# A feed-forward stage's second product: its first three row units taken one after another instead of together

## What is computed

```
def macaron_half_ffn(x, pre_g, post_g, w_gate, w_up, w_down):
    h = rmsnorm(x, pre_g)
    h = (jax.nn.silu(h @ w_gate) * (h @ w_up)) @ w_down
    return x + 0.5 * rmsnorm(h, post_g)

def swiglu_ffn(x, w_in, w_out):
    gate, up = jnp.split(x @ w_in, 2, axis=-1)
    return (jax.nn.silu(gate) * up) @ w_out
```

## Time and profile before

| what | value |
|---|---|
| time, median of 3 runs | 3608.6 us (3608.32 to 3608.63) |
| time of the profiled execution | 3610.27 us |
| its span, first to last instruction | 3608.5 us |
| PE busy with matmuls | 3288.3 us (91%) |
| DVE, ACT, POOL busy | 52%, 42%, 25% |
| mean granted TensorE clock | 0.927 of full speed |
| bytes read from HBM | 479.27 MB, 133 GB/s over the span |

### The profile page before, as it was taken

The page is one execution under the profiler, slowest core; times in us unless marked ns, Lnnn a source line. Parts: engine busy times, 40 slices in busy tenths (PEclk is TensorE's granted clock), DMA queues, the critical chain, the costliest instruction groups (busy, mean ns, idle before and its releaser), DMA issues.

```text
span 3608.5 us, 63629 instructions
## 1 busy us (share of the span) xinstructions
PE 3288.3 (91%) x27126; PEld 3135.9 (87%) x27126; DVE 1860.2 (52%) x3109; ACT 1514.5 (42%) x2540; POOL 915.4 (25%) x522
## 2 busy tenths in 40 slices
PE   7998999998798999979978999999899979987998
PEld 7997899996687999978858899899789979975898
DVE  4546455547664554365565344454435545454453
ACT  4444444444223444446454444443334443433342
POOL 2221223232342232312212222223122222220222
PEclk9998999998898999989979999999899989986899
DMA  5542354554102545533413345354224534520353
GB/s 204 175 162 80 119 185 150 185 167 148 60 3 94 181 158 187 181 127 112 138 68 129 129 152 187 133 174 152 88 82 147 175 106 153 175 86 20 107 175 117
DMA packets 133242, 484.44 MB, mean 134 GB/s; under 512 B 14815, under 2 KB 17007, under 8 KB 132255
## 3 DMA queue, kind: packets, MB, share of 16 engines
q1 hardware_dynamic: 130976, 470.25, 38.9%
q0 software_dynamic: 1984, 10.12, 0.8%
HBM read 479.27 MB, written 1.05 MB: 133 GB/s over the span
## 4 chain that ended last, share of the span: by engine, by line
PE 66%; DVE 13%; ACT 11%; issue 9%; POOL 1%; DMA 0%; SPq 0%; DVEq 0%; POOLq 0%; ACTq 0%
PE ps L174 65%; ACT hi L171 7%; DVE lo L154 2%; DVE tmp L154 1%; ACT arena L171 1%; PE ps L182 1%; DVE arena L154 1%; DVE tmp L162 1%; ACT L171 1%; DVE hfl L154 1%; POOL small L154 1%; DVE arena L162 1%; DVE yT L162 1%; DVE small L168 1%; DVE sq L154 0%
## 5 line engine op out<-in xcount | busy, mean ns | idle before, releaser
L174 PE MATMUL ps<-hh,hi 128*128 128x256 f32 (+1 forms) x4336 | 1273.3, 294 | 90.0 <-DVE hl L162 47.9
L174 PE MATMUL ps<-hh,lo 128*128 128x256 f32 (+1 forms) x4624 | 1339.6, 290 | 0.0
L154 DVE TENSOR_TENSOR lo<-raw,hi 128x1024 fp32r<-128x1024 f32 x543 | 806.4, 1488 | 1004.3 <-ACT hi L171 1004.1
L174 PE MATMUL ps<-hl,hi 128*128 128x256 f32 (+1 forms) x4336 | 1258.1, 290 | 0.0
L154 POOL TENSOR_TENSOR lo<-raw,hi 128x1024 fp32r<-128x1024 f32 x271 | 656.6, 2423 | 1946.8 <-ACT hi L171 1946.8
L171 ACT ACTIVATE hi<-raw 128x1024 fp32r<-128x1024 f32 x814 | 851.4, 1050 | 449.3 <-PE ps L174 323.7
L174 PEld LDWEIGHTS ps<-hh,hi 128*128 128x128 f32 x4336 | 847.7, 196 | 108.6 <-issue 43.6
L174 PEld LDWEIGHTS ps<-hh,lo 128*128 128x128 f32 x4624 | 901.6, 195 | 0.0
L174 PEld LDWEIGHTS ps<-hl,hi 128*128 128x128 f32 x4336 | 846.5, 195 | 0.2
L174 PE MATMUL ps<-hfh,lo 128*128 128x256 f32 (+1 forms) x1760 | 501.6, 285 | 0.0
L174 PE MATMUL ps<-hfh,hi 128*128 128x256 f32 (+1 forms) x1520 | 434.5, 286 | 11.6 <-DVE lo L154 8.9
(11 more groups left out here) (353 smaller groups left out, 3914.0 us busy)
## 6 DMA issues: line engine op xcount, KB each, us to landing
raw<-in_l_ffn_w_gate SPq DMA_DIRECT2D x88, 512.0 KB, 3.7
raw<-in_l_ffn_w_up SPq DMA_DIRECT2D x88, 512.0 KB, 3.8
raw<-in_l_ffn_w_down SPq DMA_DIRECT2D x88, 512.0 KB, 3.7
raw<-in_g SPq DMA_DIRECT2D x88, 512.0 KB, 3.7
raw<-in_u SPq DMA_DIRECT2D x88, 512.0 KB, 3.6
raw<-in_d SPq DMA_DIRECT2D x88, 512.0 KB, 3.7
raw<-in_ffn_w_gate SPq DMA_DIRECT2D x44, 512.0 KB, 3.7
raw<-in_ffn_w_up SPq DMA_DIRECT2D x44, 512.0 KB, 3.7
```

What stands on the lines that cost most here:

```text
L154: return self.e.tensor_tensor(o, a, b, op)
L174: return self.e.matmul(o, a, b, start=first, stop=final, skip_group_check=loose)
```

## The change

The list of groups loses its first group of three; all units but the last three are taken singly. For a feed-forward stage (nk = 22) that is 19 single units and a last group of three. For nk = 8 nothing changes.

```
     def pe(self, pe):
         K, T, nk = self.K, self.T, self.nk
-        ends = nk > 8
-        groups = [range(3)] * ends + [(k,) for k in range(3 * ends, nk - 3)] + [range(nk - 3, nk)]
+        groups = [(k,) for k in range(nk - 3)] + [range(nk - 3, nk)]
         for ks in groups:
             for n in range(8):
                 if self.free and ks[0] == 0:
                     pe.wait_ge(*self.free(n))
```

## The result

| | before | after |
|---|---|---|
| median | 3608.6 us (5 runs, 3605.65 to 3609.22) | 3625.21 us (5 runs, 3620.86 to 3628.32) |
| span of the profiled execution | 3608.5 us | 3619.1 us |
| mean granted clock in it | 0.927 | 0.924 |

The ratio is 1.0045, 95% interval [1.003, 1.006]: slower by 16.6 us, outside the range, and beyond the 7.2 us taken as measurable. The profiled execution of after is the shortest of its five runs (3620.86 us) and that of before, a run by itself, took 3610.27 us, so the two spans differ by 10.6 us where the medians differ by 16.6.

A forecast was written before the change was run, and what follows sets the result against it. PE's row of matmuls was taken as the bound, PE busy 91% of the span. Removed waits -18.65, new holes +17.6 and clock falls +3.6 gave +2.6 us, so 3611.2 us was forecast, range 3605.5 to 3616.

The forecast's parts named there:

- The two waits for conversions: Heads of second halves: PE's waits for DVE to convert d1 and d2 (0.44 and 2.36 us in stage 1) would go.
- the wait for mul(21): PE would reach the last product after 18 matmuls instead of 54; holes of 3.64 (stages 1 to 3) and 5.43 us (stage 4).
- The sum at full clock: Ten second halves: new holes of 17.6 us replace 18.65 us, so one us is won if the clock stays up.
- B: Rival: DVE reaches the last product earlier, so the holes vanish; 3591 us, chance 0.20 for C, 0.09 for D, 0.64 for A, B 0.03.
- C: Rival: the new holes bring no fall of the clock; 3607.6 us, chance 0.20.
- E: Rival: going through all banks with every unit costs time, at half clock 57 us in all; 3665 us, chance 0.01.
- D: Rival: the lower clock lasts longer, 6.70 us in each of four falls, costing 3.3 us each; 3621 us, chance 0.09.
- The clock's cost within the ten stretches: Falls behind the new holes: 1.6 us for stage 4, 1.0 each for two of stages 1 to 3; 3.6 us, bounds 0 to 6.8.
- two nearest rows: Profile rows with idle times of 3.41 and 3.59 us, each followed by half clock for 3.30 us; used to forecast falls.
- A: The forecast case: the wait moves from the conversions to the last product and is about as long; 3611.2 us, chance 0.64.
- such shifts: Other idle times fall differently against the clock when their stages shift by a few us; 1 to 2 us in the range.
- the sum -18.65 + 17.6 + 3.6: Old waits removed, new holes at full clock, and clock falls in the second halves; together +2.6 us.

The follow-up runs named there:

- after_filled: The kernel after, with 30 (stage 4: 46) unread matmuls filling the holes of stages 1 to 4; 3617.1 us against 3608.98 of before, ratio 1.002.
- delay_19: The kernel before, with 19 added matmuls (2.2 us pure delay) at the head of stage 5's second half; 3617.42 us against 3608.98, ratio 1.0023.
- delay_29: The kernel before, with 29 added matmuls at the head of stage 5's second half; 3613.22 us against 3610.09, ratio 1.001.
- only_without_hole: The kernel before with the new order in stages 5, 6, 7 and 9 alone; 3609.85 us against 3609.28, ratio 1.0002.
- only_stage_4: The kernel before with the new order in stage 4 alone; 3619.94 us against 3608.98, ratio 1.003.

## Why the prediction was wrong

**What held.** Where each hole goes, and how long it is. The two waits for conversions vanished, the wait for mul(21) came up behind the 18th matmul: 3.31 us idle where "3.4" was forecast, 5.22 for 5.2, and 0.35 and 0.42 in stages 8 and 10 where "about 0.5" stood. The product ended at 5.61 and 7.45 us (forecast 5.61 and 7.40). Stages 5, 6, 7 and 9 did not change. The sum at full clock, -1.0, measured -1.17 by after_filled. Rivals B, C and E did not happen. D, a longer fall in the four stretches, did in part: in stages 3 and 4 the clock stayed down for 6.8 us, about the length that D names, which cost 2.5 and 2.1 us.

**A term that was too small.** The clock's cost within the ten stretches: forecast 3.6 us (1.6 for stage 4 and 1.0 for two others), measured 660.03 - 653.96 = 6.1 us: 1.5, 0.0, 2.5 and 2.1 in stages 1 to 4. Together this is inside the bound of 6.8, but the falls of stages 3 and 4 were each over the 1.7 allowed for one, because they lasted 6.8 us, of which PE worked 5.5 and 4.7. That of stage 1 came 0.4 us behind the end of the idle time, so all of its 3.4 us slowed matmuls. The prediction had said of its two nearest rows that "the fall came while PE still stood". For the first of them this is a misreading: PE went on at 1585.63, and the clock was 1.00 until 1586.66. This term alone would have given +4.9 us, no change that can be measured.

**The step that failed.** "The range takes in A and C with their bounds and 1 to 2 us for such shifts", and the 0.02 that the forecast gave to other idle times falling differently against the clock (it was not even taken off: 0.64 + 0.20 is the 0.84 of "same"). I had read the clock only where instructions moved, and costed the rest of the program at nothing beyond the sum of the delays: the sum -18.65 + 17.6 + 3.6 has no term for it. The runs show about 12 us there (16.6 in the median less the 4.9 that the stretches grew in the trace), more than the change costs in its own stretches. Three such places are read out: the mixers between stages 5 and 6 (+4.8 in after, +4.8 in delay_19, +0.3 in delay_29), that behind stage 3 (466.7 us in three traces with the new order in stages 1 to 3; with the old one there 463.9 to 464.1 in six traces, and 468.0 in one, only_without_hole, so the same kernel up to there can also lose in this place), and the stretch behind stage 4 (135.8 with its hole, 134.5 without). The forecast's sign, +2.6, was right, by the clock's cost in the stretches. But its range gave shifts of either sign about the same weight, and the old order in stage 4, with no delay behind it, gave the cheap case between stages 5 and 6 in all four traces that have it, so there a shift had nothing to win.

The Trainium skill's page "TensorE: Matmul & The Clock Gate", section "HAM oscillation — how this bites in real kernels", says that a long idle gap between matmuls brings the engine back to the lower clock. The prediction took this to mean that all four new holes would bring it down. Three did. Stage 2 of after, idle for 3.30 us at a clock of 1.00 throughout, did not; its twin in stage 3, idle for 3.31 us, did.

**What stays open.** Stages 1 to 3 cost 5.5 us in the median, while their stretches cost 0.7 in the trace and the mixer behind stage 3 2.6. Of the rest, and of the +8.1 of after_filled, most lies in the traces in the mixer between stages 1 and 2 (321.34 and 326.60 us). But this mixer takes 314.9 to 326.6 us from trace to trace, with either order; it took 325.66 in delay_19, where nothing ahead of it was changed. One trace a kernel can't say whether its mean has moved. And why the old order arrives in the cheap case so reliably is only half answered. The traces show where it is settled: in the six in which stage 4 has the old order, the first fall behind the start of stage 4 comes 70.2 to 70.3 us after it in each, whether the mixer ahead of stage 4 had taken 464.0, 466.7 or 468.0 us. So in these traces what happened further ahead is evened out by then, and only a change of stage 4 or behind it reached the mixers between stages 5 and 6. How it is evened out is argued from the traces, not shown: a fall in a hole that ends with a stretch of half clock may bring different starts to the same distance, since stage 3 took 66.9 to 67.1 us in all seven traces with the old order there, and stage 2 66.8 to 67.1 in six of them, while the mixer ahead of stage 2 had taken 314.9 to 325.7.

## What to carry to other kernels

Before moving a wait on PE, look what else stands behind it in order: here, in stages 1 to 3, the change took waits of 3.1 us for conversions out and set one of 3.5 us for the last product in their place, where both could be avoided by doing only the six early banks first. When PE is the bound and the clock falls at idle times, what a shift of a few us costs is settled by what it meets further on, here 6 us on top of a 2.2 us delay: read every stage of two or three executions of the kernel before, and give a range as wide as their mixers differ. Keeping PE busy through a hole with matmuls whose result nobody reads took about 8 us off; their number was chosen so that they end with the hole, and the stretches became no longer by them.

## What the runs showed of the hardware

The same 60 matmuls took 7.02 us at a granted clock of 1.00 and 10.16 at 0.66, with PE busy throughout in both, and which of the two it was depended on whether a delay set some 230 us earlier was 2.2 or 3.3 us long. At the time of the prediction I would not have expected a longer pure delay (3.3 us, +3.1 in the median) to be cheaper than a shorter one (2.2 us, +8.4). Nor that one hole of 5.2 us in 3608, in place of two shorter ones, can cost 0.3% (only_stage_4, +11.0), nearly as much as the spread of thirty runs of the kernel before (0.4%).
